# Up products of the first feed-forward stages as three single-pass products of twelve-bit parts

## The chip, the cores and the metric

The kernel runs on one core of one Trainium2 chip. The metric is the device time of one execution in microseconds. The time shown for the kernel before is the median of three runs, and beside it there is one execution that the hardware profiler recorded.

## The reference, cut to what matters

A batch of one with 256 tokens of width 1024 goes through two layers, and then through a third block with a mixture of 32 experts. Everything is float32. Each of the two layers begins with a feed-forward stage, and has a second one at its end:

```
def swiglu(x, w_up, w_down):
    a, b = jnp.split(x @ w_up, 2, axis=-1)
    return (jax.nn.silu(a) * b) @ w_down

x = layer_norm(ALPHA * x + 0.5 * swiglu(x, ffn1_up[i], ffn1_down[i]), ln1_g[i], ln1_b[i])
```

`w_up` is 1024 x 5632 (two times 2816), `w_down` is 2816 x 1024. The change touches the product `x @ w_up` of the first of the two stages in each layer, in all but its first unit.

## The kernel before, in words

**Layout.** Activations lie transposed: `x` is 128 partitions x 8 chunks x 256 tokens, where chunk k holds the features 128k to 128k + 127. A product takes a block of 128 x 128 weights as the stationary operand and one chunk of 128 x 256 of `x` as the moving one, and sums over the 8 chunks in PSUM. The compiler makes of each float32 product two passes, each with its own weight load, so that a product stands in the trace as two MATMUL and two LDWEIGHTS records.

**Units.** Weights come in units of 2 MB, each 8 chunks x 512 columns, into `ring`, which has two slots that units take in turn. An up unit n holds 256 columns of the first half of `w_up` and the 256 columns of the second half that belong to them, in two transfers of 1 MB each. A stage has eleven up units (`UP1` 0 to 10) and then eight down units. TensorE works a unit off in two banks of the PSUM tensor `acc`: bank 0 holds two column blocks of the first half (those that get the silu), bank 1 the two of the second half. `acc` has four banks, so units of even and odd number take turns (`abank`).

**Around a unit.** `product` (L840 is its matmul) waits for its pair of banks to be free (`group_open` on `acc_free`) and for its unit to have landed (`unit_landed`), and then issues 4 column blocks x 8 chunks. `acc_done` counts up after each bank. ScalarE (`silus`, L1619 and L1624) waits for bank 0 and writes its silu into `silu`. VectorE (`hidden`; the call of its helper `tt` is L1957) waits for the silu and for bank 1, multiplies them into the hidden chunks in `big`, and sets the banks free. The SyncE queue (`up`, L618) asks for a unit once both banks of the unit two before it are done. Unit 0 of a stage is worked off by `product_halves` (L857), first for the left 128 tokens and then for the right 128, chunk by chunk as the layer norm before it lets go of `x` (ScalarE, L1644). The other ten units are a loop of five steps with two units each. The down products (`down_part`, L892) begin when the hidden chunks of all eleven units are there.

**Order and other work.** The order on each engine is the program's order; there is no planner. `mix`, the other four banks of PSUM, is used for the layer norm's sums (L943) ahead of and behind the up units. GpSimd works on the products of the modulation, in the second feed-forward stage of each layer, in the buffer `area`, and counts up `area_free` at its end; ScalarE and VectorE wait for that after the layer norm of the first stage. `prepare` makes the rotary tables once, behind layer 0's up units. The third block streams the experts' weights (L1497, L1513); its gather and return products are L1459 and L1470.

Of the kernel before, what the change touches and what calls it, by code (L numbers as in the profile page):

```python
# [7 lines left out]
F32 = mybir.dt.float32  # L8
# [7 lines left out]
P = 128  # L16
# [28 lines left out]
ORDER = (0, 2, 3, 1)  # L45

# [103 lines left out]
def mixed_blocks(nc, io):  # L150
    CC, NCONST = io["const_cols"], io["consts"].shape[1] - 2048
    ctx = ExitStack()
    with ctx:
# [43 lines left out]

        ring = sb("ring", [P, 2, UNIT])
        big = sb("big", [P, 32, T])
        res = sb("res", [P, DC, T])  # L200
        silu_rope = sb("silu_rope", [P, 8, T])
        branch = sb("branch", [P, HEADS, 2, T])
        tn = sb("tn", [P, DC, T])
        zp = sb("zp", [P, 4, 2, PADT])
        zz = sb("zz", [P, DC, 2, T])
        tables = sb("tables", [P, 2048])
        area = sb("area", [P, AREA])
# [156 lines left out]
        landed = [sem("unit_landed_0"), sem("unit_landed_1")]  # L364
        half_used = sem("half_used")
# [19 lines left out]
        ple_landed = sem("ple_landed")  # L385
# [93 lines left out]
        merged2_ready = sem("merged2_ready")  # L479
# [68 lines left out]

        def unit_landed(eng, L, r, i=0):

            n = turn_of(L, r)
            eng.wait_ge(landed[n % 2], (L * (RINGED // 2) + (n // 2 + 1) + i) * 32)
# [36 lines left out]

        def bc(a, n):  # L590

            return a.unsqueeze(1).to_broadcast([a.shape[0], n, a.shape[1]])
# [5 lines left out]
        def _(sp):  # L598
# [13 lines left out]

            def up(L, w, r, c):

                v = view(L, r).rearrange("p (k c) -> p k c", c=UC)
                for half in range(2):
                    cc = bass.ds(c * 256 + half * D_FF, 256)
                    sp.dma_start(v[:, :, half * 256:half * 256 + 256], w[:, L * DC:L * DC + DC, cc]) \  # L618
                        .then_inc(landed[turn_of(L, r) % 2], 16)

            def down(L, w, r, half, g):
                if r in APART:
                    v, s = down_apart, down_landed
                else:
                    v, s = view(L, r)[:, 0:11 * 256].rearrange("p (k c) -> p k c", c=256), landed[turn_of(L, r) % 2]
                for k0, k1 in ((0, 6), (6, 11)):
                    k = L * FC + 11 * half
                    sp.dma_start(v[:, k0:k1, :], w[:, k + k0:k + k1, g * 256:g * 256 + 256]).then_inc(s, 16)

            def square(L, w, r, c0, n=UC):  # L630

                v = view(L, r).rearrange("p (k c) -> p k c", c=UC)
                for k0 in (0, 4):
                    sp.dma_start(v[:, k0:k0 + 4, 0:n], w[:, L * DC + k0:L * DC + k0 + 4, c0:c0 + n]) \
                        .then_inc(landed[turn_of(L, r) % 2], 16)


            def ffn(L, up_w, down_w, r0, a0):
# [6 lines left out]
                with sp.Fori(0, 5) as i:  # L645
                    banks(L, b0 + i * 4)
                    up(L, up_w, r0 + 1, i * 2 + 1)
                    banks(L, b0 + 2 + i * 4)
                    up(L, up_w, r0 + 2, i * 2 + 2)
# [15 lines left out]
            for L in range(LAYERS):  # L665
# [30 lines left out]
                for n in range(2):  # L696
# [3 lines left out]
                    for m in range(2):  # L700
                        k = L * 8 + 2 * ORDER[2 * n + m]
                        sp.dma_start(v[:, m], w_br[:, k:k + 2, :]).then_inc(landed[turn_of(L, r) % 2], 16)
# [5 lines left out]
                sp.dma_start(ple_apart, w_ple[:, L * 2:L * 2 + 2, :]).then_inc(ple_landed, 16)  # L708
# [11 lines left out]
            def plain(w, r, c0, n=UC):  # L720
                v = view(L, r).rearrange("p (k c) -> p k c", c=UC)
                for k0 in (0, 4):
                    sp.dma_start(v[:, k0:k0 + 4, 0:n], w[:, k0:k0 + 4, c0]).then_inc(landed[r % 2], 16)
# [36 lines left out]
            for n in range(3):  # L760
# [3 lines left out]
                for k in (0, 2):  # L764
                    sp.dma_start(v[:, k:k + 2, :], w_br2[:, 4 * ORDER2[n] + k:4 * ORDER2[n] + k + 2, :]).then_inc(landed[r % 2], 16)
# [10 lines left out]
            with sp.Fori(0, last_round) as q:  # L776
# [7 lines left out]
                sp.wait_ge(merged2_ready, 4)  # L784
# [39 lines left out]
        def _(pe):  # L824
# [39 lines left out]


# [9 lines left out]
            def ffn(L, r0, a0, n, between=None):  # L875
# [6 lines left out]
                with pe.Fori(0, 5) as i:  # L882
                    product(L, r0 + 1, a0 + 1, xs, cols, i=i)
                    product(L, r0 + 2, a0 + 2, xs, cols, i=i)
# [204 lines left out]
            for L in range(LAYERS):  # L1089
# [62 lines left out]
                pe.wait_ge(p_landed, (L + 1) * 16)  # L1152
                pe.wait_ge(ple_landed, (L + 1) * 16)
# [1653 lines left out]
```

## Time and profile before

| | us |
|---|---|
| median of 3 runs | 2826.15 |
| lowest and highest run | 2821.91 and 2826.17 |
| the profiled execution, its own time | 2819.91 |
| span of its trace, first to last instruction | 2818.2 |
| TensorE busy | 2761.2 (98%) |
| VectorE busy | 576.5 (20%) |
| ScalarE busy | 423.5 (15%) |
| mean granted TensorE clock | 0.992 |

The page gives the busy time of each engine, then the span in 40 slices with the busy share in tenths, then the chain of work that ended last. A group of instructions is told by its line, engine, operation, buffers and shape. Matmul records overlap: a record of 379 ns may start every 216 ns, so the pace is read from a count of records over a stretch without gaps, and not from the length of one.

### The profile page before, as it was taken

How to read it: one execution, taken by the hardware profiler on the slowest of the kernel's cores; microseconds unless marked ns; L12 is line 12 of the kernel's file. 1: busy time of each engine (PE TensorE's matmuls, PEld its weight loads, DVE VectorE, ACT ScalarE, POOL GpSimd, SP SyncE). 2: the span in 40 equal slices, each digit the busy share in tenths (PEclk: the TensorE clock that was granted, in tenths of full speed). 3: DMA queues.
4: the chain of work that ended last, by engine and by line, in shares of the span. 5: the costliest groups of instructions: out<-in, count | busy, mean ns of one | idle time of the engine just before them, and what ended most of it. 6: DMA issues, size and time to landing. Idle time of an engine off the chain costs nothing.

```text
span 2818.2 us, 35740 instructions
## 1 busy us (share of the span) xinstructions
PE 2761.2 (98%) x14607; PEld 2035.1 (72%) x14607; DVE 576.5 (20%) x1171; ACT 423.5 (15%) x945; POOL 237.1 (8%) x130
## 2 busy tenths in 40 slices
PE   7999999999999999999999998989999999999998
PEld 7889888988998898888889887864444444444443
DVE  0022214300110022243001324311211212121212
ACT  0001120200010021201001224121111111121111
POOL 0000100481000001004800100000000000000000
PEclk9999999999999999999999999989999999999999
DMA  6444333575444443345754533459999999999999
GB/s 206 149 157 165 137 124 135 213 255 171 144 149 162 142 158 120 132 153 215 251 200 147 198 137 115 179 215 386 428 427 428 427 428 427 428 427 427 428 427 391
DMA packets 264675, 705.10 MB, mean 250 GB/s; under 512 B 12676, under 2 KB 154960, under 8 KB 214672
## 3 DMA queue, kind: packets, MB, share of 16 engines
q1 hardware_dynamic: 254416, 664.71, 60.9%
q0 software_dynamic: 9520, 36.41, 3.4%
q10 hardware_dynamic: 656, 2.78, 0.3%
q8 instruction: 64, 1.05, 0.1%
q14 instruction: 19, 0.16, 0.0%
HBM read 699.61 MB, written 6.60 MB: 251 GB/s over the span
## 4 chain that ended last, share of the span: by engine, by line
PE 90%; DMA 6%; DVE 1%; DVEq 1%; SPq 1%; ACT 0%; issue 0%; ACTq 0%
PE acc L840 34%; PE acc L1497 14%; PE acc L892 11%; PE acc L1513 7%; PE acc L1459 4%; DMA ring<-in_w 4%; PE acc L857 3%; PE acc L1331 3%; DMA ring<-in_ffn_up 2%; PE mix L1488 2%; PE acc L1384 1%; PE acc L1470 1%; PE acc L1130 1%; PE acc L1144 1%; PE acc L1350 1%; PE mix L943 1%
## 5 line engine op out<-in xcount | busy, mean ns | idle before, releaser
L840 PE MATMUL acc<-x,ring 128*128 128x256 f32 x4224 | 917.2, 379 | 3.3 <-DMA ring<-in_ffn_up 3.3
L840 PEld LDWEIGHTS acc<-x,ring 128*128 128x128 f32 x4224 | 801.0, 190 | 114.2 <-DMA ring<-in_ffn_up 4.5
L892 PE MATMUL acc<-big,ring 128*128 128x256 f32 (+1 forms) x1408 | 269.8, 353 | 2.7 <-DVE big L1957 2.7
L892 PEld LDWEIGHTS acc<-big,ring 128*128 128x128 f32 x1408 | 241.1, 190 | 32.2 <-DVE big L1957 3.9
L1497 PE MATMUL acc<-ring,zz 128*64 128x512 f32 x992 | 228.1, 600 | 5.4 <-DMA ring<-in_w 3.4
L1497 PEld LDWEIGHTS acc<-ring,zz 128*64 128x64 f32 x992 | 67.7, 137 | 143.5 <-issue 124.0
L1957 DVE TENSOR_TENSOR big<-silu_rope,acc 128x512 f32 (+1 forms) x44 | 30.2, 687 | 574.9 <-PE acc L840 537.0
L1459 PEld LDWEIGHTS acc<-area,zz 128*128 128x128 f32 x1056 | 123.6, 196 | 27.5 <-issue 27.5
L2602 DVE COPY zz<-acc 128x512 f32<-128x512 f32 x32 | 22.1, 691 | 582.2 <-PE acc L1497 582.2
L1656 ACT ACTIVATE zz<-acc 128x512 f32<-128x512 f32 x66 | 39.3, 597 | 635.0 <-PE acc L1497 587.3
L1459 PE MATMUL acc<-area,zz 128*128 128x64 f32 x1056 | 128.2, 281 | 1.4 <-DVE area L2587 1.4
L1497 PE MATMUL acc<-big,zz 128*64 128x512 f32 x528 | 124.6, 593 | 0.0
L1513 PE MATMUL acc<-big,area 128*64 128x512 f32 x496 | 118.5, 598 | 0.0
L857 PE MATMUL acc<-x,ring 128*128 128x128 f32 x768 | 89.0, 278 | 16.0 <-DMA ring<-in_ffn_up 16.0
L1624 ACT ACTIVATE silu_rope<-acc 128x512 f32<-128x512 f32 x40 | 23.9, 597 | 519.9 <-PE acc L840 519.9
L857 PEld LDWEIGHTS acc<-x,ring 128*128 128x128 f32 x768 | 88.4, 194 | 16.2 <-issue 16.0
L1497 PEld LDWEIGHTS acc<-big,zz 128*64 128x64 f32 x528 | 38.0, 138 | 75.7 <-issue 75.6
L840 PE MATMUL acc<-tn,ring 128*128 128x256 f32 x416 | 90.3, 379 | 0.3 <-DMA ring<-in_w_in 0.3
L840 PEld LDWEIGHTS acc<-tn,ring 128*128 128x128 f32 x416 | 79.0, 190 | 11.7 <-issue 1.0
L1331 PE MATMUL acc<-tn,ring 128*128 128x256 f32 x384 | 85.4, 381 | 0.8 <-DMA ring<-in_w_in 0.8
L2682 POOL TENSOR_TENSOR area<-area,cond 128x4096 f32<-128x4096 f32 x12 | 84.3, 7026 | 14.4 <-DMA area<-in_w_ada 14.2
L1911 ACT ACTIVATE zz<-acc,mod,gains 128x64 f32<-128x64 f32 x264 | 81.5, 414 | 22.0 <-PE acc L1459 11.1
(457 smaller groups left out, 2384.1 us busy)
## 6 DMA issues: line engine op xcount, KB each, us to landing
big<-in_w SPq DMA_DIRECT2D x129, 1024.0 KB, 19.3
ring<-in_w SPq DMA_DIRECT2D x128, 1024.0 KB, 20.6
ring<-in_ffn_up SPq DMA_DIRECT2D x88, 1024.0 KB, 7.1
ring<-in_w_in SPq DMA_DIRECT2D x72, 1024.0 KB, 7.0
tables<-in_w SPq DMA_DIRECT2D x33, 1024.0 KB, 17.1
branch<-in_w SPq DMA_DIRECT2D x33, 1024.0 KB, 18.7
silu_rope<-in_w SPq DMA_DIRECT2D x32, 1024.0 KB, 19.6
res<-in_w SPq DMA_DIRECT2D x32, 1024.0 KB, 19.8
```

The source lines that it names most:

```text
L840: mm = pe.matmul(abank(a, b)[:, n * T:n * T + T], w[:, k, cols[j]:cols[j] + P], rhs(k), start=k == 0, stop=k == nk - 1)
L857: mm = pe.matmul(abank(a, j // 2)[:, c0:c0 + P], w[:, k, cols[j]:cols[j] + P], x[:, k, half(h)], start=k == 0 and j % 2 == 0, stop=k == DC ...
L892: mm = pe.matmul(out, w[:, k, c * P:c * P + P], rhs(kk), start=opens and kk == 0, stop=kk == FC - 1, skip_group_check=not opens)
L1331: mm = pe.matmul(abank(a, b)[:, n * T:n * T + T], w[:, k, (2 * b + n) * P:(2 * b + n) * P + P], rhs(k), start=k == 0, stop=k == DC - 1)
L1459: mm = pe.matmul(X_BANK[:, k * C_SLOT:(k + 1) * C_SLOT], htm[:, b, k * P:k * P + P], sel[:, b, :], start=b == 0, stop=b == NB - 1)
L1488: mm = pe.matmul(mix[:, m // 2, (m % 2) * T:(m % 2) * T + T], y[lo:lo + 64, c * P:c * P + P], back[lo:lo + 64, :], start=False, stop=True, ...
L1497: mm = pe.matmul(H_BANK[j // 2][lo:lo + 64, :], x_slot[:, k, :], wbuf[n][:, j * UC:j * UC + UC], start=k == 0, stop=k == DC - 1)
L1513: mm = pe.matmul(Y_BANK[lo:lo + 64, :], hT[:, at, :], w[:, kk, half * UC:half * UC + UC], start=k == 0, stop=k == DC - 1)
L1656: return act.activation(dst, src, ACT.Copy)
L1911: c = act.activation(x_slot[:, k, :], X_BANK[:, k * C_SLOT:k * C_SLOT + C_SLOT], ACT.Identity, bias=mod[:, 24 + k:25 + k], scale=gains[:, ...
L1957: return v.tensor_tensor(out, a, b, op)
L2682: g.tensor_tensor(w, w, cond[:, :].unsqueeze(2).to_broadcast([P, DC, UC]), ALU.mult)
```

## The change

In the first feed-forward stage of both layers, units 1 to 10 are computed in another way. Chunks 0 to 5 (`SPLIT` = 6) of weights and of `x` are each cut into an upper and a lower part of twelve bits or fewer, which the type float32r can hold exactly and which TensorE is meant to multiply in a single pass. Chunks 6 and 7 stay plain float32.

- ScalarE scales a half unit of weights by 1 - 2^-13 and rounds it to float32r: the upper part `wg`. For `x` it makes `xg` in the same way, and `xk` with the scale 2^12 more.
- VectorE subtracts the upper part from the weights, in place in the ring (`wl`, the view `ring_parts`), and makes a third operand `wk` from both; for `x` it makes `xl` and `xk` once in each layer.
- TensorE issues, for each block of 128 columns and each of the six chunks, `wg` x `xg` and `wl` x `xl` into a bank of `acc`, and `wk` x `xk` into a bank of `mix` (`kbank`), where the plain products of chunks 6 and 7 have gone ahead of them.
- ScalarE copies each bank of `mix` into `joined`, and VectorE adds 1 + 2^-12 times the bank of `acc`. The silu is then taken from `joined[0]`, and the hidden chunk is made from the silu and `joined[1]`.

All parts lie over memory that is idle in the stage (`over` makes a view at the address of the next buffer). ScalarE and SyncE now have the units written out instead of a loop of five, and so has VectorE; TensorE keeps its loop. The two transfers of every unit in the kernel get a semaphore each (`landed` and `landed_2`), and for units 2 to 10 the queue asks for each half once its own bank is done. Three semaphores are merged into others, and ScalarE waits for `area_free` ahead of the stage as well.

```
+        wg, wk = area_parts[:, 0], area_parts[:, 1]
+        xg, xl, xk = branch_parts[:, 0:SPLIT, :], zp_parts[:, 0:SPLIT, :], big_parts[:, 24:24 + SPLIT, :]
+        joined = [big[:, 30:32, :], big[:, 22:24, :]]
+        NSPLIT = 1 + 20
...
+                    banks(L, b0)
+                    up(L, up_w, r0 + 1, 1)
+                    for n in range(2, 11):
+                        for hf in range(2):
+                            banks(L, b0 + 2 * (n - 2) + hf + 1)
+                            up_half(L, up_w, r0 + n, n, hf)
...
+            def split_product(L, u, i):
+                r, a = UP1 + u, G_UP1 + u
+                group_open(pe, L, a, i)
+                w, wl = (m[:, turn_of(L, r) % 2, :].rearrange("p (k c) -> p k c", c=UC) for m in (ring, ring_parts))
+                for b in range(2):
+                    half_landed(pe, L, r, b, i)
+                    for c in range(2):
+                        c0 = (2 * b + c) * P
+                        for k in range(SPLIT, DC):
+                            pe.matmul(kbank(a, b)[:, c * T:c * T + T], w[:, k, c0:c0 + P], x[:, k, :],
+                                      start=c == 0 and k == SPLIT, stop=False, skip_group_check=True)
+                    pe.wait_ge(k_ready, L * NSPLIT + (2 * u + b) + i * 4)
+                    for c in range(2):
+                        c0, ts = (2 * b + c) * P, slice(c * T, c * T + T)
+                        for k in range(SPLIT):
+                            pe.matmul(abank(a, b)[:, ts], wg[:, b, k, c * P:c * P + P], xg[:, k, :],
+                                      start=c == 0 and k == 0, stop=False, skip_group_check=True)
+                            pe.matmul(abank(a, b)[:, ts], wl[:, k, c0:c0 + P], xl[:, k, :],
+                                      start=False, stop=k == SPLIT - 1, skip_group_check=True)
+                            mm = pe.matmul(kbank(a, b)[:, ts], wk[:, b, k, c * P:c * P + P], xk[:, k, :],
+                                           start=False, stop=k == SPLIT - 1, skip_group_check=True)
+                    mm.then_inc(acc_done, 1)
...
+            def upper(L, n, hf):
+                half_landed(act, L, UP1 + n, hf)
+                act.activation(wg[:, hf], half_unit(L, n, hf, ring), ACT.Copy, scale=NEARER).then_inc(g_ready, 1)
+            def split_silus(L):
+                act.wait_ge(area_free, L + 1)
+                act.wait_ge(x_ready, 16 + 48 * L)
+                upper(L, 1, 0)
+                act.activation(xg, x[:, 0:SPLIT, :], ACT.Copy, scale=NEARER)
+                act.activation(xk, x[:, 0:SPLIT, :], ACT.Copy, scale=NEARER * STEP).then_inc(g_ready, 1)
+                upper(L, 1, 1)
+                bank_done(act, L, G_UP1, 0)
+                act.activation(silu[:, G_UP1 % 2], abank(G_UP1, 0).rearrange("p (c t) -> p c t", c=2), ACT.Silu).then_inc(silu_ready, 1)
+                for n in range(1, 11):
+                    a = G_UP1 + n
+                    bank_done(act, L, a, 0)
+                    act.wait_ge(h_ready, L * FC + n)
+                    copy(joined[0], kbank(a, 0).rearrange("p (c t) -> p c t", c=2)).then_inc(k_summed, 1)
+                    if n < 10:
+                        upper(L, n + 1, 0)
+                    act.wait_ge(a_joined, L * 10 + n)
+                    act.activation(silu[:, a % 2], joined[0], ACT.Silu).then_inc(silu_ready, 1)
+                    bank_done(act, L, a, 1)
+                    copy(joined[1], kbank(a, 1).rearrange("p (c t) -> p c t", c=2)).then_inc(k_summed, 1)
+                    if n < 10:
+                        upper(L, n + 1, 1)
...
+            def lower(L, n, hf):
+                w, l, g = half_unit(L, n, hf, ring), half_unit(L, n, hf, ring_parts), wg[:, hf].bitcast(F32)
+                v.wait_ge(g_ready, L * NSPLIT + (1 if n == 1 and hf == 0 else 2 * n + hf))
+                tt(l, w, g, ALU.subtract)
+                v.drain()
+                v.scalar_tensor_tensor(out=wk[:, hf], in0=g, scalar=-1.0 / STEP, in1=l.bitcast(F32), op0=ALU.mult, op1=ALU.add) \
+                    .then_inc(k_ready, 1)
+            def split_hidden(L):
+                lower(L, 1, 0)
+                v.wait_ge(g_ready, L * NSPLIT + 2)
+                v.scalar_tensor_tensor(out=xl, in0=x[:, 0:SPLIT, :], scalar=STEP, in1=xk.bitcast(F32), op0=ALU.mult, op1=ALU.subtract)
+                v.drain()
+                tt(xk, xg.bitcast(F32), xl.bitcast(F32), ALU.subtract).then_inc(k_ready, 1)
+                lower(L, 1, 1)
...
+                for n in range(1, 11):
+                    a = G_UP1 + n
+                    for b in range(2):
+                        bank_done(v, L, a, b)
+                        v.wait_ge(k_summed, L * 20 + (2 * (n - 1) + b + 1))
+                        o = v.scalar_tensor_tensor(out=joined[b], in0=abank(a, b).rearrange("p (c t) -> p c t", c=2), scalar=1.0 + 1.0 / STEP,
+                                                   in1=joined[b], op0=ALU.mult, op1=ALU.add)
+                        if b == 0:
+                            o.then_inc(a_joined, 1)
+                        else:
+                            v.drain()
+                            v.wait_ge(silu_ready, L * FC + (n + 1))
+                            tt(big[:, 2 * n:2 * n + 2, :], silu[:, a % 2], joined[1], ALU.mult).then_inc(h_ready, 1)
+                            v.drain().then_inc(acc_free[a % 2], 1)
+                        if n < 10:
+                            lower(L, n + 1, b)
```

## Rows read from the trace of the kernel before

**Rows 1.** The page: busy time, TensorE's clock in 40 slices, the chain by engine.

```profile
PE 2761.2 (98%) x14607; PEld 2035.1 (72%) x14607; DVE 576.5 (20%) x1171; ACT 423.5 (15%) x945; POOL 237.1 (8%) x130
...
PEclk9999999999999999999999999989999999999999
PE 90%; DMA 6%; DVE 1%; DVEq 1%; SPq 1%; ACT 0%; issue 0%; ACTq 0%
PE acc L840 34%; PE acc L1497 14%; PE acc L892 11%; PE acc L1513 7%; PE acc L1459 4%; DMA ring<-in_w 4%; PE acc L857 3%; PE acc L1331 3%; DMA ring<-in_ffn_up 2%; PE mix L1488 2%; PE acc L1384 1%; PE acc L1470 1%; PE acc L1130 1%; PE acc L1144 1%; PE acc L1350 1%; PE mix L943 1%
```

**Rows 2.** Windows: span, PE, PEld, DVE, ACT, POOL busy, clock, DMA share, GB/s.

```profile
32.00:170.00 138.00, 138.00 (x640) 121.17 (x638) 6.87 (x10) 6.15 (x12) 0.00 (x0) 1.00 0.46 158
796.00:934.00 138.00, 137.91 (x639) 121.05 (x638) 6.87 (x10) 5.97 (x10) 0.00 (x0) 1.00 0.47 158
```

**Rows 3.** Chain that ended last, around layer 1's first stage: start, us, what.

```profile
795.77 138.15 PE acc L840 x640
...
934.07 0.70 DVE big L1957
934.76 0.04 issue
```

**Rows 4.** Timeline of TensorE, passes over 128 columns: start, us, group.

```profile
242.03 2.62 PE L892 MATMUL acc<-big,ring 128*128 128x128 f32 x22
244.48 5.08 PE L892 MATMUL acc<-big,area 128*128 128x128 f32 x44
249.39 1.95 PE L857 MATMUL acc<-x,ring 128*128 128x128 f32 x16
```

**Rows 5.** Timeline of TensorE in the third block, passes over 64 columns.

```profile
1910.46 3.79 PE L1459 MATMUL acc<-area,zz 128*128 128x64 f32 x32
```

**Rows 6.** Groups of ScalarE by form: busy and mean ns, idle before.

```profile
L1624 ACT ACTIVATE silu_rope<-acc 128x512 f32<-128x512 f32 x40 | 23.9, 597 | 519.9 <-PE acc L840 519.9
L1656 ACT ACTIVATE res<-mix 128x1536 f32<-128x1536 f32 x2 | 2.9, 1450 | 1.4 <-PE mix L1041 1.4
```

**Rows 7.** Groups of VectorE by form.

```profile
L1957 DVE TENSOR_TENSOR big<-silu_rope,acc 128x512 f32 x40 | 27.5, 687 | 529.2 <-PE acc L840 529.2
L1957 DVE TENSOR_TENSOR area<-area 128x1024 f32<-128x1024 f32 x3 | 3.7, 1223 | 2.0 <-ACT area L1841 1.9
L2418 DVE SCALAR_TENSOR_TENSOR area<-mix,res 128x512 f32<-128x512 f32 x4 | 2.5, 683 | 7.9 <-PE mix L1252 7.9
L2399 DVE SCALAR_TENSOR_TENSOR zz<-zz,head_gain,mix 128x1024 f32<-128x1024 f32 x2 | 2.5, 1278 | 9.6 <-PE mix L1202 9.6
L1957 DVE TENSOR_TENSOR area<-area,s_sums 128x2048 f32<-128x2048 f32 x1 | 2.3, 2293 | 0.1
```

**Rows 8.** Timeline of VectorE and ScalarE around layer 1's unit 0.

```profile
773.28 0.29 DVE L2086 COPY lnmu<-mix 128x128 f32<-128x128 f32 x1 [3.76 <-PE mix L943]
773.65 0.29 DVE L1957 TENSOR_TENSOR lnvar<-lnmu 128x128 f32<-128x128 f32 x1
...
786.78 3.19 ACT L1644 ACTIVATE x<-tn,vec 128x128 f32<-128x128 f32 x8 [1.80 <-DVE tn L1957]
```

**Rows 9.** Timeline of GpSimd: one of its large operations, its last issue, its next work.

```profile
548.64 7.03 POOL L2682 TENSOR_TENSOR area<-area,cond 128x4096 f32<-128x4096 f32 x1
...
643.80 0.60 POOL L2689 DMA_DIRECT2D ada_sums<-branch  x1 [0.56 <-issue]
993.46 0.20 POOL L2698 MEMSET zp<- 128x128 f32 x1 [349.06 <-DMA wukv<-in_mla_w_ukv]
```

**Rows 10.** Instructions of line L2331: duration least/median/most, first and last start.

```profile
L2331 DVE SCALAR_TENSOR_TENSOR res<-res,x x2: 8648/9194/9741, 549.2 to 1314.6; 128x2048 f32<-128x2048 f32 x2
```

**Rows 11.** Up transfers (line L618): around layer 1's start, then the last of the beginning.

```profile
DMA to landing us min/median/max: 5.1/6.2/7.8
...
L618 SPq DMA_DIRECT2D ring<-in_ffn_up x1: 5758/5758/5758, 7.4 to 7.4; - x1
DMA to landing us min/median/max: 19.5/19.5/19.5
```

More of the change, by code:

```diff
@@ L194, in mixed_blocks, with over @@
         PADT = T + 16
+        def over(name, shape):
+            with nc.sbuf_tensor(name, shape, F32R) as parts:
+                return parts
+        ring_parts = over("ring_parts", [P, 2, UNIT])
         ring = sb("ring", [P, 2, UNIT])
+        big_parts = over("big_parts", [P, 32, T])
         big = sb("big", [P, 32, T])
@@ L206, in mixed_blocks @@
         tables = sb("tables", [P, 2048])
+        area_parts = over("area_parts", [P, 2, 2, SPLIT, 256])
         area = sb("area", [P, AREA])
@@ L644, in ffn @@
                 up(L, up_w, r0, 0)
[L645 to L649, printed above, removed]
+                if r0 == UP1:
+                    banks(L, b0)
+                    up(L, up_w, r0 + 1, 1)
+                    for n in range(2, 11):
+                        for hf in range(2):
+                            banks(L, b0 + 2 * (n - 2) + hf + 1)
+                            up_half(L, up_w, r0 + n, n, hf)
+                else:
+                    with sp.Fori(0, 5) as i:
+                        banks(L, b0 + i * 4)
+                        up(L, up_w, r0 + 1, i * 2 + 1)
+                        banks(L, b0 + 2 + i * 4)
+                        up(L, up_w, r0 + 2, i * 2 + 2)
                 rd = r0 + 11
@@ L721, in plain @@
                 v = view(L, r).rearrange("p (k c) -> p k c", c=UC)
[L722 to L723 removed]
+                for k0, s in ((0, landed), (4, landed_2)):
+                    sp.dma_start(v[:, k0:k0 + 4, 0:n], w[:, k0:k0 + 4, c0]).then_inc(s[r % 2], 16)
             w1 = io["w1_2"].rearrange("l e (k p) c -> p (l e k) c", p=P)
@@ L882, in ffn @@
                 with pe.Fori(0, 5) as i:
-                    product(L, r0 + 1, a0 + 1, xs, cols, i=i)
-                    product(L, r0 + 2, a0 + 2, xs, cols, i=i)
+                    for u in (1, 2):
+                        if n == 0:
+                            split_product(L, u, i)
+                        else:
+                            product(L, r0 + u, a0 + u, xs, cols, i=i)
                 nth = 0 if r0 == UP1 else FC // 2
@@ L2137, in _ @@
             for L in range(LAYERS):
-                hidden(L, G_UP1)
+                split_hidden(L)
                 if L == 0:
```

81 lines of the change are left out of this document (52 added, 29 removed).

## The prediction

> **What bounds the kernel now.** I read the page first. TensorE is busy for 98% of the span, its clock is granted in full nearly throughout, and the chain of work that ended last is 90% TensorE, with the line of the plain products (L840) alone at 34% [rows 1]. Then the windows over the two stretches that the change rewrites, the ten up units that follow unit 0 of each layer's first feed-forward stage: 138 us each, TensorE busy for all of it, VectorE for 7 us, ScalarE for 6 us, the DMA engines for 47%, GpSimd not at all [rows 2]. So the stretch costs exactly what TensorE costs, and the other engines have about 130 us to spare. The chain of waits across layer 1's stage agrees: one unbroken piece of 138.15 us for 640 records, then under a microsecond in which VectorE makes the last hidden chunk, then the down products [rows 3].
>
> The 640 records are ten units of 64: 32 products (4 column blocks by 8 chunks), each in two passes. A pass is 138.15/640 = 215.9 ns and a unit 13.82 us [rows 3].
>
> **TensorE after the change.** Per unit, chunks 6 and 7 stay plain: 4 x 2 x 2 passes x 215.9 ns = 3.45 us. The other 24 products (48 passes, 10.36 us) are removed and 24 x 3 = 72 single passes take their place. Everything hangs on the price of one, r, which no row shows; the bounds are rows of the passes that there are. A plain pass over 256 columns takes 215.9 ns [rows 3]. A plain pass over 128 columns takes 111 ns: 44 records in 5.08 us, less 0.17 us by which the last record's modelled end runs over into the next group (244.48 + 5.08 against 249.39), and 22 in 2.62 us less the same give (2.62 - 0.17)/22 = 111 too [rows 4]. A pass over 64 columns still takes about (3.79 - 0.17)/32 = 113 ns [rows 5]. So streaming costs 0.84 ns a column in a plain pass, and loading 128 weight columns costs 111 to 113 ns and is hidden behind the streaming when that is longer. Two passes of two streams each make four partial products of about 108 ns; a single-pass product should be one of them: one load, and 256 columns at half the price, 108 ns. The load then sets the pace and r = 111 ns, the row that it is nearest to, because it asks of load and stream what the 128-column pass asks. The lower end is the stream alone, 108 ns; the upper end is 216 ns, if a single pass streams no faster than a plain one or hides no load (113 + 108 = 221, the same within 3%).
>
> So a unit is 3.45 + 72 x 0.111 = 11.44 us, 2.38 us less; over 20 units the change takes out 47.5 us. The break-even is r = 141 ns (there the unit saves 0.22 us, what the edges below cost). Switching between the two kinds (four times a unit) I cost at nothing, as the semaphore waits already in the stream cost nothing at 215.9 ns a record; if each switch drained TensorE, the 0.16 us by which a 379 ns record outlasts its 216 ns pace would give 0.16 x 80 = 13 us.
>
> The Trainium skill has a rule that speaks against this change: "TensorE: Matmul & The Clock Gate", Part 3, The mechanism, says that a weight load overlaps matmuls in flight only when it goes to another row group. All products here use all rows, so by that rule each single pass would pay load and stream one after the other. The trace disagrees for plain passes, whose 111 ns hold both. The same page (Back-to-back issue gap) gives N/2.4 + 2.5 ns, an estimate of 109 ns for r and of 50 us for the saving.
>
> **The splitting work, and whether it hides.** Each half unit (6 chunks x 256 columns = 1536 elements a partition) now needs one ScalarE scaling and two VectorE operations before its split products; each bank needs one more ScalarE copy and one VectorE join. ScalarE: 1.45 us for 1536 elements, 0.60 for 512 [rows 6]. VectorE: a two-input operation takes 1.22 us for 1024 elements and 2.29 for 2048, so 1.76 us for 1536; the scalar-tensor-tensor form took 1.28 for 1024, so at most 1.81; a join is 0.68 and the product with the silu 0.69 [rows 7]. A drain between dependent operations leaves a gap of 0.08 us [rows 8], a hop from engine to engine 0.04 [rows 3].
>
> Chain for half 0 of the next unit, from the end T of a unit's first bank: copy 0.60, scaling 1.45, subtraction 1.76, drain, second part 1.78, hops: 5.8 us. The join runs on VectorE while ScalarE scales. TensorE meanwhile runs the second bank (5.72 us) and the plain products of the next first bank (1.73 us): 7.45 us of cover, 1.6 us to spare. For half 1 the chain starts behind copy 0.60, join 0.68, silu product 0.69 and two drains: 2.2 + 3.6 = 5.8 us against the same 7.45. VectorE's load per unit is 4 x 1.77 + 2 x 0.68 + 0.69 + gaps = about 9.6 us of 11.44, ScalarE's 2 x 1.45 + 3 x 0.60 = 4.7 us. So it hides; without cover each unit would pay 2 x 5.8 us. What is late next, if a chain runs over, is TensorE at its wait for the lower parts, and behind it in its queue every split product of that bank.
>
> One row speaks against: L2331 took 9.2 us for 2048 elements, four times the usual price [rows 10]. It ran at 549.2 us, beside GpSimd's large tensor operation of 548.64 us [rows 9]. GpSimd does nothing from 643.8 to 993.5 us, nor in the first stage [rows 2, 9], so the price isn't taken.
>
> **Transfers.** The weight bytes are the same. A half unit is now asked for when its own bank is done, 5.7 us apart instead of both after the second bank, and is needed by ScalarE about 12 us later; a transfer of one half lands in 5.1 to 7.8 us [rows 11]. Cost nothing, with 4 us of cover. The queue of SP holds nothing else in the stage, and the down weights follow the same banks as before. The halves' separate semaphores elsewhere (projections, down, merge, experts' stage) alter no transfer and no order. The wait for the free area moves ahead of the stage: in layer 1 GpSimd's last issue is at 643.80 us and the stage starts after 780, so nothing.
>
> **The edges.** Start of the split units in layer 1: x is complete at 786.78 + 3.19 = 789.97 us [rows 8]. ScalarE then does the first weight half and two scalings of x (4.35 us, to 794.3); VectorE the first half's two lower parts (791.5 to 795.1), then x's two (to 798.8). TensorE ends unit 0 at 795.77 [rows 3] and its plain products at 797.5: it waits 1.3 us. In layer 0, x has long landed; the last half of unit 1 lands at 7.4 + 19.5 = 26.9 us [rows 11], its scaling and lower parts take it to 32.0, and TensorE, which begins unit 1 at about 32 us [rows 2], comes to that bank a half unit later. No wait.
> End of the stage: the last bank was followed by one product (0.70 us), and now by copy, join, drain and product, 0.60 + 0.68 + 0.69 and gaps: 1.4 us more, twice: 2.8 us. The down products wait for it, and nothing covers it.
>
> **Sum.** -47.5 + 1.3 + 2.8 = -43.4 us. The profiled execution took 2819.91 us (span 2818.2) and would take 2776.5; it lies 6.2 us under the median of the runs, 2826.15, so the forecast for the median is 2783 us. Behind the stages all work is released by TensorE's own progress or data, so it shifts whole.
>
> **Rivals.**
> *A single pass costs as much as a plain one* (the one on the other side). The price is r, in every split product, and it decides from 141 ns up. At 216 ns a unit is 3.45 + 15.5 = 19.0 us, +5.2 x 20 = +103.6, with the edges +4: 2934 us. For it: no row here shows a faster stream. Against: two passes with two streams account for the plain price, and a load hides. Chance 0.10. The skill's rule above would give this result.
> *The type is not honoured* and each product still takes two passes: 72 x 0.432 + 3.45 = 34.5 us, +415 us: about 3240 us. The change would then not do what it says. Chance 0.03.
> *VectorE becomes the bound.* Its 9.6 us a unit may grow 19% before it sets the pace. At 30% more it is 12.5 us a unit, the saving 1.3 x 20 = 26, with the edges 22: 2804 us. For it: 84% busy and strict order; against: its rows repeat within 1%. Chance 0.08.
> *The saving is given back later*, because a later stage waits for something that keeps its own time, such as GpSimd's sums [rows 9] or the transfers of the experts' weights. GpSimd starts at x's release and the transfers at buffers coming free, so it would need an undiscovered wait: 2824 us. Chance 0.04.
> *The forecast*, with or without the 13 us of switches: 0.75.
>
> **How the numbers follow.** The likeliest gives 2783. r = 108 ns instead of 111 gives 4 us less, and the runs lie 4 us apart, so the range begins at 2774; switching costs (2796) and VectorE as the bound (2804) take it to 2806. Left out are 0.17 on the slow side and little below. A change of 0.2% (5.7 us) is about what a measurement of this kernel can tell from none. Faster: forecast, VectorE, and a little of the fourth: 0.84. Same: 0.03. Slower: the first two rivals: 0.13.
>
> **What the profile after would show.** The windows of both stretches are near 115 us each instead of 138, TensorE still near 100% busy, VectorE at 80% or more. The split products' line: 72 records a unit at 111 ns. TensorE's wait for VectorE's lower parts: once, 1 to 2 us, in layer 1; its wait at the first down product 2.3 us instead of 0.9. I am wrong if a single pass's pace is over 120 ns, if TensorE waits in every bank, or if VectorE's 1536-element operations come out dearer than 1.8 us.

## The result, and the profile after

The changed kernel takes 2792.89 us, median of 3 runs (2790.71 to 2792.95), against 2826.15: a ratio of 0.9885, 95% interval 0.9862 to 0.9907. The same kernel measured again (below) gave 0.9886, 0.9869 to 0.9902. So it is faster by 31 to 33 us, where 43 were forecast. The forecast of 2783 is 10 us too low; the time lies inside the range of 2774 to 2806. The profiled execution took 2790.71 us, 29.2 less than that of before.

The page of the changed kernel, the rows that answer to [rows 1], and the groups of the three split products (L936, L938, L940) and of the down products (L975):

```profile
PE 2730.6 (98%) x15087; PEld 2028.0 (73%) x15087; DVE 752.4 (27%) x1295; ACT 508.1 (18%) x1030; POOL 237.3 (9%) x130
...
PEclk9999999999999999999999999979999999999999
PE 65%; DMA 4%; DVE 1%; DVEq 1%; ACT 1%; SPq 1%; issue 0%; ACTq 0%
...
L975 PE MATMUL acc<-big,ring 128*128 128x256 f32 (+1 forms) x1408 | 271.5, 355 | 5.4 <-DVE big L2071 5.4
...
L936 PE MATMUL acc<-branch_parts,area_parts 128*128 128x256 f32 x480 | 143.1, 298 | 1.2 <-DVE big_parts L2071 1.2
...
L940 PE MATMUL mix<-big_parts,area_parts 128*128 128x256 f32 x480 | 135.7, 283 | 0.0
L938 PE MATMUL acc<-zp_parts,ring_parts 128*128 128x256 f32 x480 | 135.7, 283 | 0.0
```

Each group has 480 records, 3 x 480 = 1440 = 20 units of 72: one record for each product, so the type is honoured. TensorE waits for VectorE once, 1.2 us, in all of them. The mean of 283 ns is not the pace; that is read from the starts. The chain of this trace can be followed back only to layer 1's entry, at 777.80 us. Its 65% for TensorE therefore cannot be set beside the 90% of [rows 1], and layer 0's stage is read from windows and from the timeline.

Windows over the split units of the two layers, as in [rows 2]:

```profile
32.50:153.50 121.00, 121.00 (x882) 116.57 (x881) 83.39 (x65) 41.77 (x48) 0.00 (x0) 1.00 0.54 180
787.00:906.00 119.00, 118.68 (x868) 114.67 (x869) 86.99 (x68) 41.39 (x47) 0.00 (x0) 1.00 0.55 178
```

TensorE still sets the stretch. In layer 0 it runs from 32.55 to about 153.5 us, 121 us where 138 were; about 115 were forecast. VectorE is busy for 69 to 73% of it, ScalarE for 35%.

The chain that ended last, around the start of layer 1's split units, and at the end of its stage (compare [rows 3]):

```profile
777.80 0.77 ACT x L1761 x2
778.65 1.49 ACT area_parts L1706
780.17 1.76 DVE ring_parts L2071
782.00 1.76 DVE area_parts L2173
783.76 1.67 DVEq L2181
785.50 1.77 DVE big_parts L2071
787.32 0.39 PE acc L936
...
791.89 1.73 PE mix L930 x8
...
797.93 1.73 PE mix L930 x8
...
906.53 0.13 PE mix L940
906.68 0.60 ACT big L1701
907.38 0.69 DVE big L2193
908.15 0.70 DVE big L2071
```

A bank is 6.04 us (791.89 to 797.93, and so on through the stage) and a unit 12.08. Of a bank the eight plain passes take 1.73 us, 215.9 ns each as before, so the 36 single passes take 4.31 us: **119.7 ns each**, not 111. The first rows are the entry: layer norm, ScalarE's first weight half, VectorE's two lower parts, then its two operations on x (the first stands in the chain as the drain behind it, DVEq L2181, the second as L2071), then TensorE. The last rows are copy, join and product, 2.2 us from the last product, and the down products begin at 908.90.

The groups of the splitting work in layer 0's stretch, busy and mean ns:

```profile
L2173 DVE SCALAR_TENSOR_TENSOR area_parts<-area_parts,ring_parts 128x1536 fp32r<-128x1536 f32 x19 | 33.4, 1759 | 1.4
L2071 DVE TENSOR_TENSOR ring_parts<-ring,area_parts 128x1536 fp32r<-128x1536 f32 x18 | 31.6, 1758 | 6.7 <-ACT area_parts L1706 5.5
L1706 ACT ACTIVATE area_parts<-ring 128x1536 fp32r<-128x1536 f32 x18 | 26.6, 1476 | 0.0
L2193 DVE SCALAR_TENSOR_TENSOR big<-acc,big 128x512 f32<-128x512 f32 x19 | 13.1, 692 | 23.9 <-ACT big L1701 23.9
```

All are within 2% of the durations that the forecast took from [rows 6, 7].

One thing was in no forecast. TensorE's granted clock, in windows of 4 us behind layer 0's split units: time, busy, clock, DMA share, GB/s.

```profile
150.00:154.00 4.00, 3.50 (x30) 1.00 0.00 0
154.00:158.00 4.00, 2.25 (x8) 0.88 0.78 259
158.00:162.00 4.00, 4.00 (x14) 0.69 0.31 105
```

TensorE idles for 2.25 us ahead of the first down product, and behind that the clock is at its 1.2 GHz level for part of two windows (0.50 from 158 to 160 us): 4 x (0.12 + 0.31) = 1.7 us lost. Layer 1's end has the same idle time, 2.25 us, and its clock didn't fall.

Where the two profiled executions part, read from GpSimd's marks (its clearing of `zp` and its loads behind it in each layer), which follow the layers' progress:

| mark | before | after | difference |
|---|---|---|---|
| clearing, layer 0 | 229.33 | 215.88 | -13.5 |
| loads, layer 0 | 522.41 | 510.80 | -11.6 |
| clearing, layer 1 | 993.46 | 967.23 | -26.2 |
| loads, layer 1 | 1287.82 | 1261.91 | -25.9 |
| end | 2818.2 | 2789.0 | -29.2 |

Each stage gives 13.5 to 14.6 us, and what lies between keeps its length within 2 us. Layer 0's stage gives less partly because unit 0, which the change doesn't touch, took 16.64 us where it took 15.90, so that unit 1 began 0.8 us later (32.55 against 31.73). What lengthened it stays open.

### The profile page after: what moved, and what is told of

Same layout as the page of the kernel before. It is cut to its first block, busy times and chain, and to the rows that moved or that the text cites. A ratio compares the mean times of both kernels' runs of the same rounds, so it can differ in the third digit from the quotient of the medians.

```text
span 2789.0 us, 36880 instructions
## 1 busy us (share of the span) xinstructions
PE 2730.6 (98%) x15087; PEld 2028.0 (73%) x15087; DVE 752.4 (27%) x1295; ACT 508.1 (18%) x1030; POOL 237.3 (9%) x130
## 4 chain that ended last, share of the span: by engine, by line
PE 65%; DMA 4%; DVE 1%; DVEq 1%; ACT 1%; SPq 1%; issue 0%; ACTq 0%
PE acc L1579 15%; PE acc L895 14%; PE acc L1595 8%; PE acc L975 6%; PE acc L1541 4%; PE acc L1413 3%; DMA ring<-in_w 3%; PE mix L1570 2%; PE acc L1466 1%; PE acc L1552 1%; PE mix L930 1%; PE acc L936 1%; PE acc L938 1%; PE mix L940 1%; PE acc L912 1%; PE acc L1432 1%
## 5 line engine op out<-in xcount | busy, mean ns | idle before, releaser
L895 PE MATMUL acc<-x,ring 128*128 128x256 f32 x2944 | 640.6, 379 | 1.2 <-DMA ring<-in_ffn_up 1.2
L895 PEld LDWEIGHTS acc<-x,ring 128*128 128x128 f32 x2944 | 558.0, 190 | 79.0 <-issue 3.5
L975 PE MATMUL acc<-big,ring 128*128 128x256 f32 (+1 forms) x1408 | 271.5, 355 | 5.4 <-DVE big L2071 5.4
L975 PEld LDWEIGHTS acc<-big,ring 128*128 128x128 f32 x1408 | 242.3, 191 | 35.0 <-DVE big L2071 6.2
L936 PE MATMUL acc<-branch_parts,area_parts 128*128 128x256 f32 x480 | 143.1, 298 | 1.2 <-DVE big_parts L2071 1.2
L940 PE MATMUL mix<-big_parts,area_parts 128*128 128x256 f32 x480 | 135.7, 283 | 0.0
L938 PE MATMUL acc<-zp_parts,ring_parts 128*128 128x256 f32 x480 | 135.7, 283 | 0.0
L912 PEld LDWEIGHTS acc<-x,ring 128*128 128x128 f32 x768 | 89.1, 196 | 16.3 <-issue 16.0
L936 PEld LDWEIGHTS acc<-branch_parts,area_parts 128*128 128x128 f32 x480 | 91.8, 191 | 2.6 <-DVE big_parts L2071 1.6
L938 PEld LDWEIGHTS acc<-zp_parts,ring_parts 128*128 128x128 f32 x480 | 91.9, 191 | 1.0
L940 PEld LDWEIGHTS mix<-big_parts,area_parts 128*128 128x128 f32 x480 | 91.8, 191 | 0.0
L895 PE MATMUL acc<-tn,ring 128*128 128x256 f32 x416 | 90.4, 379 | 0.5 <-DMA ring<-in_w_in 0.5
```

The costliest lines, as they stand in the source:

```text
L895: mm = pe.matmul(abank(a, b)[:, n * T:n * T + T], w[:, k, cols[j]:cols[j] + P], rhs(k), start=k == 0, stop=k == nk - 1)
L912: mm = pe.matmul(abank(a, j // 2)[:, c0:c0 + P], w[:, k, cols[j]:cols[j] + P], x[:, k, half(h)], start=k == 0 and j % 2 == 0, stop=k == DC ...
L936: pe.matmul(abank(a, b)[:, ts], wg[:, b, k, c * P:c * P + P], xg[:, k, :], start=c == 0 and k == 0, stop=False, skip_group_check=True)
L938: pe.matmul(abank(a, b)[:, ts], wl[:, k, c0:c0 + P], xl[:, k, :], start=False, stop=k == SPLIT - 1, skip_group_check=True)
L940: mm = pe.matmul(kbank(a, b)[:, ts], wk[:, b, k, c * P:c * P + P], xk[:, k, :], start=False, stop=k == SPLIT - 1, skip_group_check=True)
L975: mm = pe.matmul(out, w[:, k, c * P:c * P + P], rhs(kk), start=opens and kk == 0, stop=kk == FC - 1, skip_group_check=not opens)
```

## The experiments

Two questions stood open: why is a single pass 119.7 ns, and does the work on the other engines cost more than its edges? The first four experiments change what TensorE does and leave the other engines as they are. A rival needs no run: that the other engines' use of the memory slows the single passes. The changed kernel's own trace has a stretch, in the last bank of layer 1's stage, in which VectorE, ScalarE and GpSimd do nothing and the DMA engines are at 1% (a window as above, with PE, PEld, DVE, ACT and POOL):

```profile
903.00:906.00 3.00, 3.00 (x27) 3.00 (x26) 0.00 (x0) 0.00 (x0) 0.00 (x0) 1.00 0.01 3
```

The single passes start 0.12 us apart there too (28 steps from 903.01 to 906.37 us), so this rival is out.

### moving128: the stream halved

```
+        pe.matmul(abank(a, b)[:, c * T:c * T + P], wg[:, b, k, c * P:c * P + P], xg[:, k, 0:P], ...)   # k = 1..5
```

> The split products of chunks 1 to 5 take only 128 of the 256 token columns (chunk 0 stays whole), so half of their results are left out. The single pass measured 119.7 ns, where I had forecast 111. If the weight load sets that pace (theory L), the narrow ones stay at 120 ns and a unit at about 12.1 us. If the stream of 256 columns sets it (theory S), they fall to the 111 ns that loading costs in plain passes, and a unit to 12 x 0.120 + 60 x 0.111 + 3.45 = 11.6 us.

It took 2785.03 us in one run; the kernel before, measured beside it, took 2823.98. Timeline of TensorE:

```profile
790.80 0.27 PE L943 MATMUL acc<-branch_parts,area_parts 128*128 128x128 f32 x1
...
791.58 0.28 PE L945 MATMUL acc<-zp_parts,ring_parts 128*128 128x128 f32 x1
```

Seven steps in 0.78 us: 111 ns, as theory S expected. The load's floor is the same in single passes as in plain ones, and at 256 columns something costs 9 ns more.

### weights64: the load halved

```
+        pe.matmul(abank(a, b)[0:64, ts], wg[:, b, k, c * P:c * P + 64], xg[:, k, :], ...)   # k = 1..5
```

> The split products of chunks 1 to 5 load only 64 of the 128 weight columns, so half of their output rows are left out. Theory L: with half the load the stream sets the pace, about 107 to 110 ns. Theory S: still 120 ns.

2785.53 us in one run.

```profile
791.10 0.28 PE L943 MATMUL acc<-branch_parts,area_parts 128*64 128x256 f32 x1
...
791.79 0.28 PE L943 MATMUL acc<-branch_parts,area_parts 128*64 128x256 f32 x1
```

Six steps in 0.69 us: 115 ns. Over whole banks, which follow one another every 5.853 us, it is (5.853 - 1.727 - 6 x 0.1197)/30 = 114 ns. Neither theory expected that: with half the load the pass is faster than 120 and still above 108. So the stream alone isn't 108 ns but about 114, and a load of full width adds the other 6.

### moving512: the stream doubled

```
+        pe.matmul(abank(a, b)[:, :], wg[:, b, k, c * P:c * P + P], xg[:, k:k + 2, :].rearrange("p k t -> p (k t)"), ...)   # k = 0, 2, 4
```

> Each split product streams two chunks of the parts of x in a row, 512 columns, and every second product is left out: half as many products, each twice as wide, 36 a unit; the sums are other ones than the reference's. Theory L (load of 120 ns, hidden under a longer stream of 0.42 ns a column): about 216 ns each, a unit 3.45 + 36 x 0.216 = 11.2 us. Theory S (0.47 ns a column): 240 ns each, a unit 12.1 us as before.

```profile
793.67 0.40 PE L938 MATMUL acc<-zp_parts,ring_parts 128*128 128x512 f32 x1
...
797.30 0.39 PE L940 MATMUL mix<-big_parts,area_parts 128*128 128x512 f32 x1
```

Sixteen steps in 3.63 us: 227 ns, 0.443 a column. That lies between theory L's 216 and theory S's 240, and 256 columns at this price are 113.5 ns, what weights64 showed. The whole took 3726.98 us, which says nothing here: the altered sums route the third block's tokens otherwise, and its largest group of products has 1984 passes instead of 992.

### bank_runs: does changing the PSUM bank cost?

```
-        for k in range(SPLIT):  wg x xg -> acc;  wl x xl -> acc;  wk x xk -> mix
+        six of wg x xg -> acc, then six of wl x xl -> acc, then six of wk x xk -> mix
```

> The same 36 products of a bank, in another order: six into the first bank with the upper parts, six with the lower parts, then six into the other bank, instead of turn by turn between the two. If the change of the PSUM bank costs the 9 ns (theory B) the pace falls to about 111 ns and the kernel by 12 us; theories L and S both expect no change, 119.7 ns.

2788.86 us in one run.

```profile
792.04 0.88 PE L939 MATMUL acc<-zp_parts,ring_parts 128*128 128x256 f32 x6
792.76 0.88 PE L942 MATMUL mix<-big_parts,area_parts 128*128 128x256 f32 x6
```

Six passes start every 0.72 us: 120 ns still. The bank is no cause.

### plain_products: the splitting work without its gain

```
-        (the three single-pass products)
+        mm = pe.matmul(abank(a, b)[:, ts], wg.bitcast(F32)[:, b, k, c * P:c * P + P], xg.bitcast(F32)[:, k, :], ...)
```

> All of the splitting, copying and joining stays, but TensorE multiplies the upper parts alone, as plain products of two passes, 64 passes a unit as before; the lower parts' products are left out, so the sums are only nearly the reference's. If the work on ScalarE and VectorE costs TensorE nothing but the edges (my account), a unit is 13.8 us and the kernel 4 to 6 us slower than the kernel before. If that work slows TensorE's passes by their shared memory (rival), the passes come slower than 215.9 ns and the kernel is 10 us or more slower.

2827.21 us (2822.47 to 2830.23, 8 runs) against 2821.72 (17 runs): ratio 1.002, interval 1.0009 to 1.0031, or +5.5 us. All scalings, lower parts, copies and joins are there. Plain passes keep their pace beside them:

```profile
810.67 5.18 PE acc L936 x24
```

That is 215.8 ns each. The trace has the changed kernel's edges (1.2 us at layer 1's entry, 2.7 at the two ends) and one fall of the clock behind layer 0's end, 5.6 us in all, near the 5.5 measured. The work beside the plain passes costs what the edges and the clock cost, and with the window above none of the missing 10 us is its price.

### split4: the size of the change

```
-        SPLIT = 6
+        SPLIT = 4
```

> Four chunks split instead of six, the sum is the same. If a single pass costs a fixed 119.7 ns and switching nothing, a unit is 32 x 0.2159 + 48 x 0.1197 = 12.65 us, 0.6 us more than with six, and the kernel 12 us slower than the changed one (about 2804 to 2805). If switching or the chain through ScalarE and VectorE held part of the time, less of the gain is lost.

2801.29 us (2800.38 to 2802.78, 4 runs): ratio 0.9928, interval 0.9912 to 0.9945, 20.4 us less. With 119.7 ns a unit should be 32 plain passes and 48 single ones, 6.91 + 5.75 = 12.65 us, and the chain of waits has its plain groups 6.33 us apart:

```profile
802.61 3.46 PE mix L930 x16
808.94 3.46 PE mix L930 x16
```

Its trace shows no wait at layer 1's entry and the same three at the stages' ends, so the edges are 2.7 us and not 3.9. 20 x (13.82 - 12.65) less 2.7 is 20.7, and 20.4 was measured: the account by pace and edges holds at another size. It is 8 to 12 us slower than the changed kernel (by the medians, by the ratios), where 12 were expected; part of the less is that it had neither the wait of 1.2 us nor the clock's fall.

### interleaved: plain and single passes mixed

```
+        three of a bank's four plain products go between the single passes: behind (c, k) = (0, 2), (0, 5) and (1, 2)
```

> Three of the four plain products of each bank are issued between the split ones, each behind nine single passes, instead of ahead of them; all sums are the same. The wait for the lower parts comes 1.3 us earlier in the bank. If switching between the kinds costs nothing and a single pass is a fixed 119.7 ns, a unit stays at 12.08 us as long as the chain has 1.3 us to spare, and the time is that of the changed kernel within 2 us. If a load can run ahead under a plain pass's longer stream (rival), up to 3 x 13 ns a bank are gained, 1.5 us in all; if switching costs, 12 more switches a unit make it slower by 12 x 20 x their price.

2793.24 us (2788.09 to 2794.6, 4 runs): ratio 0.9889, 0.9872 to 0.9905, against 0.9886 for the changed kernel beside it. The whole time cannot tell the cases apart, but the trace can. The plain products of this kernel, four groups apart:

```profile
811.12 0.60 PE L929 MATMUL mix<-x,ring 128*128 128x256 f32 x2
...
817.12 0.60 PE L929 MATMUL mix<-x,ring 128*128 128x256 f32 x2
```

A bank is 6.00 us, and so on through the stage, where the changed kernel's is 6.04. So four times as many switches cost nothing, and the rival came true: 40 ns a bank are gained, where 3 x 13 were expected of a load that runs ahead under a plain pass. That is 1.6 us over the 40 banks. The time doesn't show it because the earlier wait for the lower parts lengthens layer 1's entry from 1.2 to 2.5 us, and the clock fell behind that (1.7 us).

### four_forms: what a single pass costs by shape

```
+        W = {(0, 1): 64, (0, 2): 32, (1, 1): P, (1, 2): 64}[form]   # form = (layer, even or odd unit), k = 1..5
+        512, 256, 256 (always chunk 0) and 128 columns streamed
```

> The split products of chunks 1 to 5 take four other forms, one for each parity of the unit in each layer, and leave out or change part of the sums: layer 0, odd units: 64 weight columns, 512 moving ones; layer 0, even units: 32 weight columns, 256 moving; layer 1, odd: 128 and 256, but always the same chunk; layer 1, even: 64 and 128. So far a single pass took 119.7 ns for 128 x 256, 115 for 64 x 256, 227 for 128 x 512 and 111 for 128 x 128. Theory F: each pass streams at 0.417 ns a column and pays a fixed part beside it, 13 ns with 128 weight columns and 8 with 64, so the forms come at about 221, 112, 119.7 and 62 ns. Theory S (the stream itself is slower, 0.445 ns a column, and the weights add only where they are not hidden): 228, 114, 119.7 and 57 to 60. If the chunk's address mattered, the third would leave 119.7.

2797.12 us in one run. The first and the last of a run of records in three of the forms:

```profile
36.00 0.40 PE L953 MATMUL acc<-branch_parts,area_parts 128*64 128x512 f32 x1
...
37.85 0.40 PE L957 MATMUL mix<-big_parts,area_parts 128*64 128x512 f32 x1
...
51.23 0.28 PE L953 MATMUL acc<-branch_parts,area_parts 128*32 128x256 f32 x1
...
52.81 0.28 PE L957 MATMUL mix<-big_parts,area_parts 128*32 128x256 f32 x1
...
820.06 0.22 PE L953 MATMUL acc<-branch_parts,area_parts 128*64 128x128 f32 x1
...
820.89 0.22 PE L957 MATMUL mix<-big_parts,area_parts 128*64 128x128 f32 x1
```

The forms are 64 weight columns with 512 moving ones, 32 with 256, and 64 with 128. Eight steps in 1.85 us are 231 ns for 512 columns (over the whole stretch 230), 14 in 1.58 us are 113 for 256 with 32 weight columns (115 over longer runs), 14 in 0.83 us are 59 for 128. The same chunk over and over gave 120, so addresses have no part. The price goes with the columns, 0.44 to 0.46 ns each, and has no fixed part that a theory of overhead needs: 59 x 4 = 237 is near 230, where a fixed 8 or 13 ns would have made 221 of it. At half the load, at a quarter of it and at 512 columns with the whole load the price a column is the same within 2% (0.443 to 0.450 ns); with 128 columns it is 0.46. The whole load of 128 columns with 256 streamed lies above it, by 6 ns. That shape is the one where load (111) and stream (114) are nearly equal. Theory S has the forms right.

### after_down_first and before_down_first: the idle time ahead of the down products

The first group of down products reads the hidden chunks in order; its first half needs those of units 0 to 5 alone.

```
-        pe.wait_ge(h_ready, L * FC + nth + 11)          # ahead of the group
+        pe.wait_ge(h_ready, L * FC + nth + 6)           # ahead of the group
+        pe.wait_ge(h_ready, L * FC + nth + 11)          # ahead of its second half
```

> The changed kernel, with the wait for the last hidden chunk moved in all four feed-forward stages: the first down group waits only for the chunks of units 0 to 5, multiplies those (9.5 us), and waits for the rest then. If the ends of the stages cost what their idle time shows (2.25 us twice, 0.9 us twice) and a lowered clock behind one of them (1.7 us), the kernel gains 6 to 8 us on the changed one. If TensorE only waits elsewhere for the same, it gains under 2.

> The kernel before with the same move of the wait. Its ends are 0.9 us each in four stages: it gains 2.7 to 3.6 us on the kernel before, less than half of what the changed kernel gains by it.

On the changed kernel: 2782.85 us (2781.36 to 2783.72, 4 runs), ratio 0.9863, 0.9847 to 0.9880. That is 6 us less than the changed kernel by the ratios and 9 by the medians, and their runs don't overlap (2788.69 the lowest there). On the kernel before: 2816.12 (2814.15 to 2820.01, 10 runs), ratio 0.9987, 0.9977 to 0.9997, which is 3.7 us less by the ratio and 5.6 by the medians. So it gained at least the forecast 2.7 to 3.6 us, but not less than half of what the changed kernel gained. Its trace has the three waits of 0.9 us gone, which is 2.7; where the rest comes from stays open. On the changed kernel, the first down products in the chain, and its clock where the changed kernel's fell:

```profile
898.76 0.12 PE acc L936
899.85 25.25 PE acc L975 x117
```

```profile
154.00:158.00 4.00, 4.00 (x20) 1.00 0.94 297
158.00:162.00 4.00, 4.00 (x21) 1.00 0.20 68
```

No wait, TensorE busy throughout and its clock whole. The 5.4 us of idle time in three places (L975 in the page above) and the 1.7 of the clock make 7.1 us, and the two profiled executions differ by 8.0. This is the fastest kernel of the study, level with split7_down_first.

### after_again: the changed kernel a second time

> The changed kernel unchanged, timed with more runs and beside the others of this call. My account of its profile (20 units at 12.08 us instead of 13.82, edges +3.9, a lowered clock of about 1.7 us behind a stage's end in some executions) gives 29 to 31 us less than the kernel before.

2791.61 us (2788.69 to 2796.7, 4 runs), ratio 0.9886, 0.9869 to 0.9902, or 31 to 32 us less. Its marks agree with the first execution's within 1.1 us up to the third block (215.97, 510.72, 968.29, 1261.04); its end, 2795.0, lies 6 us later. From the last mark to the end the two executions took 1527.1 and 1534.0 us, and the kernel before, between them, 1530.4. So the third block varies by more than the stages do, and the -3.3 us that the table of marks shows behind 1262 us need be no effect of the change.

### split7_down_first: one more chunk

```
-        SPLIT = 6;  joined = [big[:, 30:32, :], big[:, 22:24, :]]
+        SPLIT = 7;  joined = [res[:, 0:2, :], big[:, 22:24, :]];  the last down weights are asked for later;  the wait moved as above
```

> Seven chunks split instead of six, on top of the moved wait for the last hidden chunks; one joined buffer and the last down weights go to other places and times so that the parts fit. TensorE: 8 x 0.2159 + 84 x 0.1197 = 11.78 us a unit, 0.3 us less, 6 us in all. The chain is 0.60 + 1.69 + 2 x 2.03 + 0.25 = 6.6 us against a cover of 5.89 + 0.86 = 6.75, and VectorE needs 11.0 of 11.78 us. If both fit, it is 4 to 6 us faster than six chunks with the moved wait; if the chain or VectorE runs over (rival), TensorE waits in every bank and the gain is gone or turns into a loss.

2783.84 us (2783.21 to 2786.77, 4 runs), ratio 0.9864, 0.9848 to 0.9881: level with six chunks and the moved wait, where it was to be faster. Its chain of waits at layer 1's entry:

```profile
779.00 2.04 DVE big_parts L2076
781.08 0.39 PE acc L939
...
782.08 0.21 PE acc L939
...
785.47 0.12 PE acc L941
...
793.77 0.86 PE mix L933 x4
...
799.67 0.86 PE mix L933 x4
```

A bank is 5.90 us, as it should be, which gives 20 x 0.28 = 5.6 us; TensorE waits in no other bank, so neither the forecast nor its rival came true. The wait at layer 1's entry was in no forecast. With 1792 instead of 1536 elements in each operation, TensorE waits 3.3 us there instead of 1.2, and behind this wait single passes start 0.21 us apart, the 1.2 GHz level, for three microseconds: 2.1 + 1.7 = 3.8 us. Two smaller losses are no clear effect of the change: unit 1 of layer 0 began 0.6 us later, and layer 0's second stage waited twice for transfers, 1.0 us in all. The marks agree: 1.9 us ahead of six chunks with the moved wait after layer 0 (209.48 against 211.42), level at the next clearing (958.30 and 958.21).

## Why the prediction was right, and where it was off

**What bounds the kernel: right.** TensorE still fills both stretches, and its pace alone sets them.

**TensorE after the change: right in kind, mis-sized in one term.** The step was "a single-pass product should be one of them: one load, and 256 columns at half the price, 108 ns. The load then sets the pace and r = 111 ns". Measured: r = 119.7 ns, a unit 12.08 us instead of 11.44, and 20 x (13.82 - 12.08) = 34.8 us instead of 47.5. These 12.7 us are more than the whole error. The load's part of the step was right (111, moving128). The stream's wasn't: a single pass streams 256 columns in about 114 ns (weights64, four_forms), and not in half a plain pass's 215.9. Two such streams would be 228, more than the plain pass takes, so "two passes of two streams each" doesn't give the price of a single one; no run shows what a plain pass consists of. So the stream sets the pace, not the load. On top come 6 ns where load and stream are nearly equal. That the load is then partly exposed fits every shape tried, and interleaved, where a plain pass ahead gives back 13 ns, fits it too; no run shows the mechanism itself.

**The condition "I am wrong if a single pass's pace is over 120 ns"** isn't met, by 0.3 ns only. The break-even at 141 was far off, which is why the sign was safe. That the time lies in the range is partly luck: the range went up to 2806 for the switches and for VectorE, which cost nothing, and the 10 us came from the pass's price, for which it left no room above 111 ns.

**Switching at nothing: right.** The plain passes kept 215.9 ns, and four times as many switches made a bank 0.04 us shorter, not longer (interleaved).

**The splitting work hides: right.** TensorE waits in no bank but the first, and plain_products shows that the work costs 5.5 us in all, edges and one fall of the clock. VectorE's share came out at 69 to 73%, not over 80: its operations cost what was said (1.76 and 0.69 us), but the unit is longer, the tenth unit splits nothing, and the gaps of the drains, counted in the 9.6 us, are not busy time.

**Transfers: right.** The split products wait for none.

**The edges: right.** Entry 1.2 us (1.3 forecast), no wait in layer 0, wait at the first down product 2.25 us (2.3 forecast), which makes 1.35 more for each layer. What was not seen is that the clock can fall behind a wait of this length: it did in layer 0, 1.7 us, and not in layer 1.

**The sum.** -34.8 + 1.2 + 2.7 + 1.7 = -29.2 us, and the two profiled executions differ by 29.2. That this meets to the tenth is chance, since the marks have another 0.8 us lost ahead of unit 1 in layer 0, 1.9 lost between layer 0's two marks (the clock fell there too, at about 460 to 466 us, in a place where it held before) and 3.3 won in the third block, which is within what after_again shows to be scatter.

**The rivals.** A single pass as dear as a plain one, the type not honoured, VectorE as the bound: all refuted by the pace. The Trainium skill's rule for it ("TensorE: Matmul & The Clock Gate", Part 3, The mechanism), that a load overlaps only another row group, doesn't hold here: 114 and 111 ns one after the other would be 225, and 119.7 were measured. The same page's formula (Back-to-back issue gap), which it states for the isolated gap of a single matmul, gives an estimate of 109 ns; the traces disagree with 119.7, and with 227 against an estimate of 216 at 512 columns. Given back later: a little of it, through the clock.

## What to carry to other kernels

A price that no row shows should be bounded by measuring the form itself where that can be done; where it can't, a resource that comes within a few per cent of another (here the load beside the stream) deserves a margin, since two nearly equal limits gave more than the larger. When a change lengthens the tail of a stage, look at what the next stage really needs first: moving one wait behind half a group of products gave back 6 to 9 us, a fifth to a quarter as much as the whole change. And a wait of two or three microseconds in a dense stream of products may cost its own length and the slower clock behind it, 1.7 us here.

## What the runs showed of the hardware

- Single-pass products (float32r) with 128 x 128 weights: 111 ns with 128 columns streamed, 119.7 with 256, 227 with 512; with 64 weight columns 59 with 128, 114 with 256 and 230 with 512; with 32 weight columns 115 with 256. Plain float32 passes over 256 columns: 215.9. The 119.7 ns are the same with VectorE and ScalarE idle and the DMA engines at 1% (the changed kernel, 903 to 906 us).
- Writing float32r costs ScalarE and VectorE what float32 does, within 2%: for 1536 elements a partition 1476 ns against the 1450 of [rows 6], and 1758 ns against 1760, an estimate between the 1223 and 2293 of [rows 7].
- The same idle time of 2.2 us ahead of the down products of a first stage was followed by 1.2 GHz in the profiled executions of the changed kernel (both, layer 0 alone), plain_products (layer 0), moving128 (both layers), moving512 and four_forms (layer 1), and in neither layer in those of bank_runs, split4, interleaved and weights64. Waits of 3.3 us (split7_down_first) and 2.5 us (interleaved) at layer 1's entry were followed by 1.2 GHz, the changed kernel's of 1.2 us was not. Each fall cost 1.7 us, and up to the third block an execution had between one (before) and four (interleaved), a difference of 5 us. What decides in the cases between stays open.
